# Routing and experts of a PEER layer: two blocks with a barrier made into one block with one ring of weight tiles

## The reference, cut to what matters

```python
q = (xf @ wq).reshape(n, PEER_HEADS, 2, PEER_HALF)
s = jnp.einsum('nhpd,hpkd->nhpk', q, subkeys).astype(jnp.float32)
s_top, i_top = lax.top_k(s, PEER_TOPK)
cand = s_top[:, :, 0, :, None] + s_top[:, :, 1, None, :]
cand_idx = i_top[:, :, 0, :, None] * PEER_NKEYS + i_top[:, :, 1, None, :]
best_s, best_j = lax.top_k(cand.reshape(n, PEER_HEADS, -1), PEER_TOPK)
expert = jnp.take_along_axis(cand_idx.reshape(n, PEER_HEADS, -1), best_j, axis=-1)
gate = jax.nn.softmax(best_s, axis=-1)
...
h = jnp.einsum('nd,nhkd->nhk', xb, u[eb]).astype(jnp.float32)
coef = (gb * jax.nn.gelu(h, approximate=False)).astype(xb.dtype)
return jnp.einsum('nhk,nhkd->nd', coef, v[eb])
```

## Time and profile before

| | |
|---|---|
| median of 3 runs | 2134.33 us (2133.69 to 2137.74) |
| profiled execution | 2130.83 us |
| its span | 2129.1 us |
| PE busy | 1919.3 us, 90% |
| VectorE (DVE) busy | 1611.2 us, 76% |
| ScalarE (ACT) busy | 758.0 us, 36% |
| GpSimd (POOL) busy | 568.9 us, 27% |
| DMA, mean | 193 GB/s |

### The profile page before, as it was taken

How to read it: one execution, slowest core, us unless ns; L and a number is a source line. 1 busy time by engine, 2 the same in 40 slices (tenths; PEclk the granted TensorE clock), 3 DMA queues, 4 the chain that set the end, 5 groups by cost and what they waited for, 6 DMA issues and landing times. The chain is left out here.

```text
span 2129.1 us, 33182 instructions
## 1 busy us (share of the span) xinstructions
PE 1919.3 (90%) x12866; PEld 1646.4 (77%) x12866; DVE 1611.2 (76%) x2830; ACT 758.0 (36%) x1114; POOL 568.9 (27%) x395
## 2 busy tenths in 40 slices
PE   5989997889998989999499999659999999999995
PEld 4968875459963479999499999648888889999994
DVE  6278993324553389999699999658888887999998
ACT  3232454432210044433255555323333333333331
POOL 2322343000000055544200000112222224656561
PEclk9988999988999999999799999879999999999997
DMA  3211231010050054444457665499999998999993
GB/s 121 76 54 50 87 125 45 1 41 3 4 199 0 0 195 137 129 133 134 140 200 251 243 231 192 176 342 351 348 363 346 359 362 298 368 383 389 384 340 120
DMA packets 169683, 410.97 MB, mean 193 GB/s; under 512 B 13504, under 2 KB 85184, under 8 KB 166352
## 3 DMA queue, kind: packets, MB, share of 16 engines
q1 hardware_dynamic: 117712, 253.41, 34.8%
q0 software_dynamic: 36864, 134.23, 17.0%
q10 hardware_dynamic: 14976, 21.50, 2.8%
HBM read 360.33 MB, written 48.76 MB: 192 GB/s over the span
## 5 line engine op out<-in xcount | busy, mean ns | idle before, releaser
L2134 PE MATMUL ps<-v_hl,coef_hl 128*128 128x512 f32 x2304 | 534.5, 392 | 39.9 <-DVE coef_hl L2168 39.9
L2134 PEld LDWEIGHTS ps<-v_hl,coef_hl 128*128 128x128 f32 x2304 | 434.3, 189 | 129.7 <-DVE coef_hl L2168 40.5
L1739 PE MATMUL ps<-h_hl,w_hl 128*128 128x384 f32 (+1 forms) x1664 | 326.9, 348 | 8.7 <-DVE h_hl L1811 8.7
L1739 PEld LDWEIGHTS ps<-h_hl,w_hl 128*128 128x128 f32 x1664 | 294.2, 190 | 19.6 <-issue 9.0
L1951 POOL DMA_INDIRECT gathered_rows<-in_u_rows,pick_index x128 | 134.6, 1052 | 611.8 <-DVE pick_hidden L1961 499.1
L2078 ACT ACTIVATE v_hl<-v_staged 128x1024 fp32r<-128x1024 f32 x128 | 135.4, 1058 | 240.7 <-PE ps L2134 193.1
L2173 DVE TENSOR_TENSOR v_hl<-v_staged,v_hl 128x1024 fp32r<-128x1024 f32 x128 | 156.6, 1223 | 70.1 <-ACT v_hl L2078 70.0
L1951 POOL DMA_INDIRECT gathered_rows<-in_v,pick_index x128 | 177.3, 1385 | 116.7 <-DVE h_tok L1970 82.9
L1640 POOL TENSOR_TENSOR w_hl<-w_staged,w_hl 128x1024 fp32r<-128x1024 f32 x56 | 143.3, 2563 | 151.2 <-ACT w_hl L1665 150.9
L1970 DVE SCALAR_TENSOR_TENSOR h_tok<-gathered_rows,pick_hidden,h_tok 128x1024 f32<-128x1024 f32 x128 | 164.3, 1283 | 9.8
L633 PE MATMUL ps<-hT_hl,w_hl 128*128 128x264 f32 (+1 forms) x1024 | 169.1, 324 | 0.0
(11 more groups left out here) (319 smaller groups left out, 2757.9 us busy)
## 6 DMA issues: line engine op xcount, KB each, us to landing
v_staged<-in_v SPq DMA_DIRECT2D x128, 512.0 KB, 8.4
w_staged<-in_stream SPq DMA_DIRECT2D x104, 512.0 KB, 3.9
dense_gates<-lot SPq DMA_DIRECT2D x24, 1024.0 KB, 4.9
gates<-dense_gates SPq DMA_DIRECT2D x16, 1536.0 KB, 13.9
w_staged<-in_w_in_t SPq DMA_DIRECT2D x40, 512.0 KB, 3.5
h1T<-in_stream SPq DMA_DIRECT2D x40, 512.0 KB, 7.1
parked_gelu<-h1T ACTq DMA_DIRECT2D x88, 192.0 KB, 2.9
coef<-parked_gelu SPq DMA_DIRECT2D x88, 192.0 KB, 5.8
```

The lines of the kernel that those rows point to most:

```text
L1739: nc.tensor.matmul(bank, w_hl[:, j % RING, 0, P * k:P * (k + 1)], h_hl[:, part, k, lo:hi], start=(k == 0 and part == 0), stop=False)
L2134: last = nc.tensor.matmul(ps[:, 2 + 2 * t + half, :], coef_hl[:, k % HLS, c, P * t:P * (t + 1)], v_hl[:, k % HLS, v, 512 * half:512 * (hal ...
```

## The change

The two functions become one, `peer`, with one block; the barrier between them goes. One ring of 4 staged tiles and one of 4 high and low pairs carry all weights, query, U and V tiles, in the order in which PE uses them (positions `V_AT`, `U_AT`): from tile 64 on, VectorE makes all low parts, GpSimd before. BETWEEN goes from 8 to 16 and GATES_AT from 4 to 12, and ScalarE copies the gates behind tile 12 of them instead of behind all. Six expert tiles stand behind the last lot, in banks 0 and 1, while the last piece of the table is stored and the gates come back. PARKED goes from 88 to 102, so that 26 tiles and not 40 are computed between sums. Of the gathered rows 24 are used in the lots as before, 12 beside the six tiles, one per k to k = 101, and 118 in the last 26 k. In the loop over k ScalarE makes the coefficients' high copy first and then the high copy of the weight tile three positions on; VectorE subtracts the weight tile one position on between the weighing and the coefficients' low part. The ring `coef` lies in memory of `h1T`.

```diff
-BETWEEN = 8
-PARKED = 4 * PEER_HEADS + BETWEEN + 2 * LOTS
-GATHER_RING, GATHERED_EARLY = 8, 24
+BETWEEN = 16
+PARKED = 4 * PEER_HEADS + BETWEEN + 2 * LOTS + 6
+GATHER_RING = 8
...
-        route(nc, a, locals())
-        experts(nc, a, locals(), out)
+        peer(nc, a, locals(), out)
...
-    GATES_AT = 4
+    GATES_AT = BETWEEN - 4
...
+    V_AT, U_AT, s = {}, {}, QUERIES + PARKED
+    for k in range(EXPERT_KEYS):
+        if k + LEAD < EXPERT_KEYS and k + LEAD >= PARKED:
+            U_AT[k + LEAD] = s
+            s += 1
+        V_AT[k] = s
+        s += 1
...
+    used_behind = [LOTS + 2 * (n + 1) for n in range(BEHIND)]
+    EARLY = used_behind[-1]
+    used_by = [EARLY + (k + 1 if k < PARKED else PARKED + (2 * PICKS - EARLY - PARKED) * (k + 1 - PARKED) // FRESH)
+               for k in range(EXPERT_KEYS)]
...
+    def freed_by(s):
+
+        s -= RING
+        if s < QUERIES + PARKED:
+            return "tile", s + 2
+        for k in V_AT:
+            if V_AT[k] == s:
+                return "sum", k + 1
+            if U_AT.get(k) == s:
+                return "tile", QUERIES + k + 2
...
+            def load_late(s):
+
+                if s < STREAMED:
+                    sp.wait_ge(late_low, s - RING - BY_POOL + 1)
+                    sp.dma_start(staged[:, s % RING, :], source(s) if s >= QUERIES + PARKED else a["stream"][s]
+                                 ).then_inc(landed[s % RING], 16)
...
+            for k in range(COEFS):
+                load_parked(k)
             for j in range(2):
                 sp.wait_ge(lot_stored[j], 16 * (LOTS // 2))
-                sp.wait_ge(act_parked[j], 16 * (PARKED // 2 + 1))
+            load_gates(0)
+            for s in range(FIRST_BEHIND, QUERIES + PARKED):
+                load_late(s + RING)
+            for k in range(EXPERT_KEYS):
+                if k + LEAD in U_AT:
+                    load_late(U_AT[k + LEAD] + RING)
+                load_late(V_AT[k] + RING)
+                if k == 1:
+                    load_gates(1)
+                if k % LOOP == LOOP - 3 and LOOP < k < EXPERT_KEYS - LOOP:
+                    load_gates(k // LOOP + 1)
+                if k + COEFS < PARKED:
+                    load_parked(k + COEFS)
...
+            def high_of(s):
+                if s < STREAMED:
+                    what, n = freed_by(s)
+                    act.wait_ge(landed[s % RING], 16 * (s // RING + 1))
+                    act.wait_ge(tile_done if what == "tile" else sum_done, n)
+                    nc.scalar.activation(w_hl[:, s % RING, 0, :], staged[:, s % RING, :], ACT.Copy).then_inc(w_high, 1)
...
             for j in range(BETWEEN):
                 expert(TOPK_TILES + j)
-                if j == 1:
+                if j == GATES_AT - 3:
                     act.wait_ge(lowered, 1)
                     nc.scalar.activation(picks[:, 2], picks[:, 2], ACT.Exp).then_inc(raised, 1)
-            act.wait_ge(picks_copied, 3)
-            nc.scalar.activation(gate_hl[:, 0, :], picksT[:, 2, :], ACT.Copy).then_inc(gate_high, 1)
+                if j == GATES_AT:
+                    act.wait_ge(picks_copied, 3)
+                    nc.scalar.activation(gate_hl[:, 0, :], picksT[:, 2, :], ACT.Copy).then_inc(gate_high, 1)
...
+            for s in range(FIRST_BEHIND, QUERIES + PARKED):
+                expert(s, behind=True)
...
+            for k in range(EXPERT_KEYS):
+                if k >= PARKED:
+                    act.wait_ge(tile_done, QUERIES + k + 2)
+                    act.wait_ge(coef_low, k - COEFS + 1)
+                    nc.scalar.activation(coef[k % COEFS], ps[:, k % 2, 0:DENSE], ACT.Gelu).then_inc(gelu_made, 1)
+                high_coef(k)
+                if k + LEAD in U_AT:
+                    high_of(U_AT[k + LEAD] + 3)
+                high_of(V_AT[k] + 3)
...
-                if n + 1 < LOTS:
-                    low(BY_POOL + TILES_A_LOT * (n + 1))
-                if n < GATHERED_EARLY:
-                    dot_rows(nc, dve, h_tok, gathering, n)
...
+                low(BY_POOL + TILES_A_LOT * (n + 1))
+                dot_rows(nc, dve, h_tok, gathering, n)
+            for n in range(BEHIND):
+                low(FIRST_BEHIND + n + 1)
+                for x in range(used_behind[n] - 2, used_behind[n]):
+                    dot_rows(nc, dve, h_tok, gathering, x)
...
                 weigh(k)
-                if f >= 0 and f + 2 < FRESH:
-                    low_u(f + 2)
-                low_v(k)
+                if k + LEAD in U_AT:
+                    low(U_AT[k + LEAD] + 1)
+                low(V_AT[k] + 1)
                 low_coef(k)
-                for n in range(used_by[k - 1] if k else GATHERED_EARLY, used_by[k]):
+                for n in range(used_by[k - 1] if k else EARLY, used_by[k]):
```

391 lines of the change are left out of this document (150 added, 241 removed).

## The result

| | before | after |
| --- | --- | --- |
| median of 4 runs each | 2134.3 us (2133.7 to 2137.7) | 2148.2 us (2145.5 to 2149.7) |
| after / before, 95% interval | | 1.0049 (1.0026 to 1.0072) |
| profiled execution, its span | 2130.8, 2129.1 us | 2145.5, 2143.8 us |

The changed kernel is 0.5% slower. I had forecast 2110 us and a range of 2086 to 2142. The time lies above the range and the sign is wrong.

The account below looks back on a forecast made before the run. TensorE was 90% busy, so gains had to come from its waits. First sums at 1397 plus 408, 20 and 254 us gave 2079 against 2103.04; 24 us off the median gave 2110 us, range 2086 to 2142.

Parts of the forecast that it names:

- Gates: Before the transposes: eight more tiles cut PE's wait for the gates from 30.2 to 1.5 us (0 to 3.1).
- Lots: Gate table's lots: start 7.9 us earlier less 1.2, PE's last product at 1360.9 instead of 1367.64, eight tiles richer.
- Behind the lots: After the last lot: six tiles (25.0 us) replace waits, 11 us waiting for a late weight tile, first sums at 1397.
- the 39.9: PE's wait before the first sums in the kernel before, two pieces (25.8 and 14.1 us), forecast as removed with the barrier.
- Plain rounds: 100 rounds of sums without a tile: 4.08 us each, 408 us, plus 20 us stalls behind twelve gates loads (5 to 50).
- Last 26 rounds: Rounds with a tile: DVE bounds at 9.27 us a round, 254 us to the tail's start (224 to 8 us more).
- Rival 1: 100 plain rounds: shorter look-ahead makes PE stall for V, deciding from 44 us on; 65 us stall, 2155 us; chance 0.12.
- rival 5: Whole change: frees waits and pays as much, 44 us of stalls, so 2134 us; chance 0.06.

Follow-up runs that it names:

- gates_whole: Changed kernel with each gates load read as 128 contiguous pieces of 12 KB, same bytes but wrong gates: 2105.6 us.
- split_gates: Changed kernel with each gates load of the rounds cut into four, spread over four rounds, the first load behind the lots left whole: 2112.8 us.
- split_all: split_gates with the first gates load also cut, a quarter ahead of each of the first four weight tiles behind the lots: 2105.8 us.
- split_late: split_gates with the first gates load also cut, its quarters behind the weight tiles behind the lots instead of ahead of them: 2115.0 us.

## Why the prediction was wrong, point by point

The forecast span was 2105.1 us, the measured one 2143.8: 38.7 us off. The parts below are 1.9 + 7.1 + 6.5 + 17.9 us, and 5.2 us of the start.

1. **Gates: right.** A wait of 1.5 us was forecast (0 to 3.1), it is 2.94. The gates came 7.3 us later than before, counted from the routing's start, where I had added 4.8 and bounded it by 6.4. Of these, 1.3 us stand ahead of the first ranking already, as they do in the second run of the kernel before, and PE came 1.3 us later too; 6.0 us lie in the last ranking, inside the bounds. Three of DVE's operations there hold them, each beside one of POOL's subtractions, of 2.40 to 3.37 us (from 1022.06, 1034.54 and 1038.67). DVE's timeline of after:

```profile
1022.59 1.96 DVE L2040 CAST keys<-top_at 128x128 f32<-128x128 uint32 x1
1034.43 4.56 DVE L2055 TENSOR_TENSOR is_place<-place,count 128x1024 f32<-128x1024 f32 x2
1039.03 4.44 DVE L2060 TENSOR_TENSOR is_place<-is_place,keys 128x1024 f32<-128x1024 f32 x2
```

   Before, with POOL idle, the same rows took 0.23, 2.36 and 2.36 us. The rule of the Trainium skill weighed there ("SBUF — State Buffer", SBUF: two separate sides) would at its worst have made the wait 17 us; the trace agrees with the lock in three places, 6.0 us, and not with its worst case.
2. **Lots: right within 1.9 us.** PE's last product ended at 1368.0, 606.9 us after the routing's start; forecast were 605.0.
3. **Behind the lots: mechanism right, size wrong, 7.1 us.** I had the tile that waits and why (the Gelu behind a copy behind a load behind the gates' return) but sized it by 14 us from the gates' issue to ScalarE, where it took 19.3 (1373.80 to 1393.11); another 1.8 us are the first tile behind the wait, 4.70 us for 2.93 (the granted clock was 0.61 there). I had taken fewer transfers as a faster landing. The timelines of SP and ACT:

```profile
1373.80 0.38 SPq L1710 DMA_DIRECT2D gates<-dense_gates  x1
1374.22 14.17 SPq L1704 DMA_DIRECT2D w_staged<-in_stream  x2
...
1393.11 1.06 ACT L1825 ACTIVATE w_hl<-w_staged 128x1024 fp32r<-128x1024 f32 x1 [20.27 <-DMA w_staged<-in_stream]
```

   The run without the six tiles shows that the gates' return takes 18.3 us of PE when nothing fills it. The gain booked for the six tiles, 25 us of work for 11 us of wait, did not exist: with and without them the kernel takes the same time. And the 14.08 us of the 39.9 that I booked with the barrier were of another kind, the U load stuck behind the second gates load: the mechanism that cost most later stood in the trace of before.
4. **Plain rounds: 6.5 us.** The stalls behind gates loads were there, one in eight rounds, and 14.5 us in all where I had 20. That the gates themselves would be late for DVE, I had not. The round was sized wrong: I took 4.08 us from 4.10 by way of the matmuls that the trace lacks, and the unbroken group shows 413.87 / 100 = 4.14. That is 6 us. Another 6 us are longer products, most of them in the first group (18.35 us for 72) and in one behind the longest wait (36.01 us for 144, the others 33.24).
5. **Last 26 rounds: the step that failed, 17.9 us.** DVE's round of 9.3 us was right, and without the two long waits the stretch is 271.9 - 18.7 = 253.2 us, the 254 of the forecast. That is a subtraction; gates_whole, which has no such wait, comes to 256 us (282.2 less 26 for the tail), split_gates only to 262. But I had applied the stall behind gates loads, found in the earlier trace rows, to the plain rounds alone; the last rounds have no term for it, and no reason is given. The same loads fall into these rounds too, and they cost more there. U and V come through the same ring of four, so one blocked issue is late for two tiles a round, and ScalarE has the Gelu of the round behind the late copy. Two of them cost 10.64 and 8.04 us. In before SP also stood behind such a load (12.32 us from 1787.72 on), with ScalarE waiting for V only 4.4 us in that whole stretch: harmless for a kernel with two rings, and no sign that it would be for one.
6. **The start of the routing,** 5.2 us, is scatter and was no step.
7. **The rivals.** Rival 1 named this side and this family of cause, a shorter look-ahead, but placed it in the plain rounds and wanted 44 us of stall there; there were 14.5. The loss was spread over the lots' end, the plain rounds and the last part, and no rival added these. By its number rival 1 (2155 us) was nearest, but with the loss in the wrong place; rival 5 (2134 us, gains and stalls equal) was 14 us short. A chance of 0.12 for slower was too little where four of the prices hung on one queue.

The sum of the parts also hid that they are not independent. Once the gates loads are cut and DVE is evened out, the tiles ahead of the gates are worth 26.7 us of the 27 that the wait lost. In the kernel as changed, the same tiles were taken from rounds that DVE bounds, where taking away a tile should save less; no run takes them away there.

A rule of the Trainium skill ("DMA: Bandwidth & Descriptors", Rules for kernel authors) asks, for bandwidth, for 1 MiB or more a DMA and to gather small transfers into large ones. The runs go the other way here: cutting 1.5 MB into four of 384 KB made the kernel 35 to 42 us faster, since what counted was the load behind. The 12 KB pieces, with the load uncut, were as good (2105.6 us), and both ways the block in the rounds is gone. Of the time to start a DMA the same page (Issuing engines are not separate DMA queues) says that it is usually small beside the transfer. The rows agree at 0.33 us, and disagree behind a gates load, with 12.13 us for one load and 14.17 us for two.

## What to carry to other kernels

When two rings become one, list every large or finely cut load on the same queue and compare the lead of the load behind it, in microseconds, with what the queue stood behind it before, in every stretch and not only in the one where it was seen. Cut such a load into parts shorter than that lead before the buffers are shared. And a tile put into a wait is won only if its own weights don't come over the thing that is waited for; a run without the filler shows this at once.

## What the runs showed of the hardware that was not expected

- An issue of one load on SP's queue took 0.33 us alone. Behind a 1.5 MB gates load it took 3.8 to 6.1 us in the plain rounds (a load of 192 KB), 3.72, 12.13 and 11.33 us in the last rounds (a weight load of 512 KB), and 14.17 us for two weight loads behind the lots. Behind a quarter of the same load it was 0.33 us in the plain rounds and 0.33 to 1.6 us in the last. The block does not grow in proportion to the bytes ahead.
- Behind the lots quarters blocked it all the same: the weight loads behind the four quarters took 0.99, 4.36, 5.74 and 2.71 us in split_all, and two of them 9.06 and 6.68 us in split_late. Why there and not in the rounds is open; in both the pieces are of 512 bytes.
- A DMA share near 1 was no sign of a limit. The same rounds moved 332 GB/s in after (share 0.96), 351 with the loads cut (1.01) and 372 with more rows (1.03).
- TensorE's clock fell after waits that look harmless. In this stretch of after, right behind the wait of 10.64 us (columns of the earlier trace rows), it was granted 0.50, that is 1.2 GHz; the same 16 matmuls took 5.46 us there and 2.93 at 2.4 GHz.

```profile
1952.00:1958.00 6.00, 5.53 (x17) 5.57 (x18) 5.54 (x6) 1.79 (x3) 0.88 (x1) 0.50 0.55 172
```

  With more rows and whole gates loads even waits of 2.5 to 5.3 us were followed by groups of 34.8 to 36.1 us for 33.24, and the mean clock of those plain rounds was 0.95, against 0.99 with the loads cut. So the 22.5 us of added waits cost 38 us.
